# Squares summed in a tree on VectorE, one ones-matmul for a chunk, in the front of a hybrid encoder layer

## What is computed

```python
def rms_norm(x, g, eps=NORM_EPS):
    xf = x.astype(jnp.float32)
    y = xf * lax.rsqrt(jnp.mean(xf * xf, axis=-1, keepdims=True) + eps)
    return (y * g.astype(jnp.float32)).astype(x.dtype)

hn = rms_norm(x, g_pre_mix)
z, xbc, dt_raw, q, k, v = jnp.split(hn @ w_in, IN_SPLITS, axis=-1)
xbc, conv_new = causal_conv(conv_buf, xbc, conv_w, conv_b)
...
mn = rms_norm(mem, g_mem)          # 256 rows
mk, mv = mn @ wk_x, mn @ wv_x
```

## Time and profile before

| | |
|---|---|
| median of three runs | 2197.03 us |
| the profiled execution | 2196.18 us, its span 2194.4 us |
| TensorE matmul busy | 2009.8 us (92% of the span), granted clock 0.946 on average |
| VectorE busy | 924.7 us (42%) |
| ScalarE busy | 508.1 us (23%) |
| GpSimd busy | 438.5 us (20%) |
| the chain that ended last | TensorE 78%, VectorE 14%, ScalarE 3%, DMA 2% |

### The profile page before, as it was taken

How to read it: one execution, slowest core, us unless ns; L and a number is a source line. 1 busy time by engine, 2 the same in 40 slices (tenths; PEclk the granted TensorE clock), 3 DMA queues, 4 the chain that set the end, 5 groups by cost and what they waited for, 6 DMA issues and landing times.

```text
span 2194.4 us, 29435 instructions
## 1 busy us (share of the span) xinstructions
PE 2009.8 (92%) x12084; PEld 1910.8 (87%) x12084; DVE 924.7 (42%) x1673; ACT 508.1 (23%) x1078; POOL 438.5 (20%) x211
## 2 busy tenths in 40 slices
PE   8989989995988799898989978999999999999996
PEld 7988979995676698797879958999999999999995
DVE  3753176672777425503433452313322322331336
ACT  5322212323555322312322322010010000001002
POOL 0000011130000042131004213332341431433330
PEclk9999999996599899999989988999999999999998
DMA  5133222124002410013320121111110110110132
GB/s 179 58 121 106 89 89 85 62 79 149 1 1 89 166 39 30 19 58 141 128 87 29 58 87 39 39 39 39 39 52 27 49 48 21 58 39 30 49 106 86
DMA packets 63045, 148.71 MB, mean 68 GB/s; under 512 B 4288, under 2 KB 34368, under 8 KB 61376
## 3 DMA queue, kind: packets, MB, share of 16 engines
q1 hardware_dynamic: 33952, 103.53, 14.0%
q10 hardware_dynamic: 28960, 43.24, 5.7%
HBM read 123.31 MB, written 23.44 MB: 67 GB/s over the span
## 4 chain that ended last, share of the span: by engine, by line
PE 78%; DVE 14%; issue 3%; ACT 3%; DMA 2%; ACTq 0%; SPq 0%; DVEq 0%
PE bank L198 22%; PE bank L202 21%; PE bank L201 21%; PE bank L249 3%; DVE at_sm L1858 2%; DVE NLf L258 2%; PE bank L964 2%; PE bank L975 1%; DVE acc L1629 1%; PE bank L934 1%; DMA qkr<-out_k 1%; DVE ATT L1877 1%; DVE hid_l L2085 1%; PE bank L843 1%; PE bank L641 1%
## 5 line engine op out<-in xcount | busy, mean ns | idle before, releaser
L201 PE MATMUL bank<-NL,w_hi 128*128 128x384 f32 x1800 | 610.9, 339 | 0.0
L198 PE MATMUL bank<-NH,w_hi 128*128 128x384 f32 x1608 | 549.3, 342 | 36.7 <-DVE hr L2083 12.4
L202 PE MATMUL bank<-NH,w_lo 128*128 128x384 f32 x1608 | 545.0, 339 | 0.0
L483 POOL TENSOR_TENSOR w_hi<-w_raw,one 128x1024 fp32r<-128x1024 f32 x90 | 183.4, 2038 | 1219.2 <-PE bank L198 1097.2
L201 PEld LDWEIGHTS bank<-NL,w_hi 128*128 128x128 f32 x1800 | 342.0, 190 | 1.5
L198 PEld LDWEIGHTS bank<-NH,w_hi 128*128 128x128 f32 x1608 | 305.2, 190 | 40.4 <-DVE hr L2083 13.0
L202 PEld LDWEIGHTS bank<-NH,w_lo 128*128 128x128 f32 x1608 | 305.2, 190 | 0.0
L485 POOL TENSOR_TENSOR w_lo<-w_raw,w_hi 128x1024 fp32r<-128x1024 f32 x90 | 228.4, 2538 | 7.1
L2083 DVE TENSOR_TENSOR hr<-sg,bank 128x384 f32<-128x384 f32 x66 | 36.6, 554 | 433.3 <-PE bank L202 433.3
L198 PE MATMUL bank<-hid_h,w_hi 128*128 128x384 f32 x528 | 179.0, 339 | 16.0 <-DVE ACC L2094 14.6
L2094 DVE TENSOR_TENSOR ACC<-ACC,bank 128x384 f32<-128x384 f32 x240 | 131.8, 553 | 115.8 <-PE bank L202 115.8
(11 more groups left out here) (319 smaller groups left out, 2941.2 us busy)
## 6 DMA issues: line engine op xcount, KB each, us to landing
w_raw<-in_wall SPq DMA_DIRECT2D x130, 512.0 KB, 3.3
cK<-in_cmk SPq DMA_DIRECT2D x8, 1024.0 KB, 7.0
cV<-in_cmv SPq DMA_DIRECT2D x8, 1024.0 KB, 5.0
H<-in_xT SPq DMA_DIRECT2D x5, 1536.0 KB, 12.5
scratch_h<-H ACTq DMA_DIRECT2D x3, 1536.0 KB, 6.0
Hback<-scratch_h ACTq DMA_DIRECT2D x3, 1536.0 KB, 10.5
out_y<-Hback ACTq DMA_DIRECT2D x3, 1536.0 KB, 6.0
Kb<-in_kc SPq DMA_DIRECT2D x6, 512.0 KB, 9.0
```

The source lines that it names most:

```text
L198: m = mm(out, ah, bh, start=(i == 0), stop=False)
L201: mm(out, ah, bl, start=False, stop=False)
L202: m = mm(out, al, bh, start=False, stop=(i == n - 1))
L483: pool.tensor_tensor(whi[s][:], raw[s % 2][:], bc(one[:, 0:1], [P, WI]), ALU.mult).then_inc(w_hi, 1)
```

## The change

The eight squares of a chunk are no longer summed by eight accumulating ones-matmuls. `front_sum` adds them on VectorE, in place, in a tree of three additions (4 + 4 blocks, 2 + 2, 1 + 1), and `front_pe` issues one ones-matmul on the block that is left. This is done for the three chunks of x and for the memory; the norms later in the program keep `pre_pe`. A new semaphore (`norm_front_sum`) joins the tree to the ones-matmul; a few unused names of semaphores go.

```diff
+        def front_sum(dve, p, w):
+
+            dve.wait_ge(n_sq, 4 * p + 4)
+            s = g("msq" if p == P_MEM else f"fsq{p % 2}")
+            for n in (4, 2):
+                dlink(dve, TT(s[:, 0:n, 0:w], s[:, 0:n, 0:w], s[:, n:2 * n, 0:w], ALU.add))
+            TT(s[:, 0, 0:w], s[:, 0, 0:w], s[:, 1, 0:w], ALU.add).then_inc(n_sum, 1)
+
+        def front_pe(pe, p, w):
+
+            pe.wait_ge(n_sum, p + 1)
+            if p:
+                pe.wait_ge(n_std, p)
+            mm(B[7][:, 0:w], ones[:, :], g("msq" if p == P_MEM else f"fsq{p % 2}")[:, 0, 0:w], start=True,
+               stop=True).then_inc(n_pc, 4)
...
                 if c:
-                    pre_pe(pe, P_MIX + c - 1, NC)
+                    front_pe(pe, P_MIX + c - 1, NC)
...
                         if m == 2 and c == 0:
-                            pre_pe(pe, P_MIX + 2, NC)
+                            front_pe(pe, P_MIX + 2, NC)
                         if m == 2 and c == 1:
-                            pre_pe(pe, P_MEM, MEM)
+                            front_pe(pe, P_MEM, MEM)
...
             weight_low(dve, 2)
-            n_low(2)
+            front_sum(dve, P_MIX, NC)
+            x_low(2)
             weight_low(dve, 3)
+            front_sum(dve, P_MIX + 1, NC)
+            front_sum(dve, P_MIX + 2, NC)
...
             conv(0)
             weight_low(dve, 5)
+            front_sum(dve, P_MEM, MEM)
             pre_dve(dve, P_MEM, g("mraw"), g("mraw")[:], g("mlo")[:], g("mhi")[:], G_MEM, MEM)
```

More of the change, by code:

```diff
@@ L162, in build @@
         ld_x0 = [sem(f"ld_x0_{i}") for i in range(2)]
-        s_past = sem("conv_past")
+        s_past, n_sum = sem("conv_past"), sem("norm_front_sum")
         w_raw = [sem(f"w_raw_in{i}") for i in range(2)]
@@ L370, in build @@
         a_lo, a_oc, b_kn, b_pn = sem("att_qk_low"), sem("att_out"), sem("smp_new_keys"), sem("smp_new_values")
-        a_tr, a_tre, a_S, a_nb, a_exp, a_att, a_T, a_Te, a_pv, a_o, a_on, a_yt, a_yte = (
+        a_tr, a_tre, a_S, a_nb, a_exp, a_att, a_T, a_Te, a_pv, a_on, a_yt, a_yte = (
             sem("att_" + n) for n in ("qk_trans", "qk_copy", "scores", "max", "exp", "probs", "ptrans", "pcopy", "pv",
-                                      "ocopy", "onorm", "otrans", "oout"))
+                                      "onorm", "otrans", "oout"))
         ld_kb = [sem(f"ld_kc{i}") for i in range(DB // 2)]
-        b_q, b_S, b_nb, b_exp, b_p, b_T, b_Te, b_pv, b_o, b_ot, b_ote = (
-            sem("smp_" + n) for n in ("qbd", "scores", "max", "exp", "probs", "ptrans", "pcopy", "pv", "ocopy", "otrans",
-                                      "otok"))
+        b_q, b_S, b_nb, b_exp, b_p, b_T, b_Te, b_pv, b_o = (
+            sem("smp_" + n) for n in ("qbd", "scores", "max", "exp", "probs", "ptrans", "pcopy", "pv", "ocopy"))
         x_qh, x_ql, mk_h, mk_l = (sem("x_" + n) for n in ("q_high", "q_low", "k_high", "k_low"))
@@ L1574, in _, with x_low @@
             dve.wait_ge(ld["vec"], 16)
-            def n_low(c):
+            def x_low(c):
                 for i in range(4):
@@ L1584, in _ @@
             weight_low(dve, 0)
-            n_low(0)
+            x_low(0)
             weight_low(dve, 1)
-            n_low(1)
+            x_low(1)
             weight_low(dve, 2)
-            n_low(2)
+            front_sum(dve, P_MIX, NC)
+            x_low(2)
             weight_low(dve, 3)
+            front_sum(dve, P_MIX + 1, NC)
+            front_sum(dve, P_MIX + 2, NC)
             dve.wait_ge(ld["row"], 16)
```

## The result

The changed kernel takes 2205.71 us (median of its runs, 2202.03 to 2215.01), the kernel before 2197.0 in the same rounds: ratio 1.0041, 95% interval 1.0029 to 1.0054. I had forecast 2192.4, at most 2197.6. The profiled execution took 2205.78 us (span 2204.0). One of the sixteen executions took 3542.77 us at a granted clock of 0.765; it is left out of the range and of the ratio and hardly moves the median.

A forecast was written before the change was run, and what follows sets the result against it. The front was taken as bound by TensorE up to chunk 2's root, then by VectorE's queue to 114.60. Shift 4.3 + clock 0.3 = 4.6 us: profiled 2196.18 becomes 2191.6, median 2192.4 us; range 2188.0 to 2197.6.

The forecast's parts named there:

- VectorE's part: Additions put into VectorE's queue: some 3.3 us a tree, 2.4 for the memory's, 12.4 us for all four.
- Step by step: Front traced through TensorE, ScalarE and VectorE: root of chunk 2 8.7 us earlier, memory's norm 4.3 us earlier.
- The wait that the change adds: Behind the memory's tree, VectorE has nothing for 2.0 us during ones-matmul, ScalarE steps and hand-overs; TensorE waits 10.6 us before.
- Does TensorE become late: Before x5: TensorE still waits for the low part, some 2 us instead of 6.2, so the 4.3 us reach 114.60.
- The clock: TensorE's half clock behind the pause at 114.60 and two later pauses; balance put at 0.3 us gained.
- rival B: Behind 114.60 the clock stays up, so 3.0 us come back too: 7.3 us gained, 2189.7 us; chance 0.20.
- The failed step: After 114.60, loads, splits and matmuls start each other, so the 4.3 us shift stays to the end.
- Rival D: Slower: memory's tree and wait, 4.4 us on VectorE's queue, not earned back; 2201.4 us, about 2203 with half clock; chance 0.09.
- The chain of waits in the front, because the change touches nothing later: What the prediction examined for the bound: waits up to 114.60, where TensorE has 6.2 us of slack beside VectorE's queue.

The follow-up runs named there:

- run 1: Changed kernel plus eight always-met waits (four instructions) on TensorE before the memory's ones-matmul; 2180.39 us, ratio to the kernel before 0.9913.
- run 6: Changed kernel plus 223 met waits (111 instructions), so the feed-forward loop begins at the same instruction number as in the kernel before; 2188.49 us, ratio 0.9947.
- run 7: Changed kernel plus 144 met waits (72 instructions), so the loop begins 70 instructions behind the start of a 16 KB piece; 2189.74 us, ratio 0.9959.
- run 2: Kernel before plus met waits in two TensorE pauses, so the loop begins 253 instructions behind a 16 KB piece's start; 2213.55 us, ratio 1.0064.
- run 5: Kernel before plus 299 met waits (149 instructions), so the loop begins 2 instructions behind a 16 KB piece's start; 2182.38 us, ratio 0.9932.
- run 8: Kernel before plus 156 met waits (78 instructions), so the loop begins 187 instructions behind a 16 KB piece's start; 2197.47 us, ratio 1.0004.
- run 4: Kernel of run 1 with the memory's tree on VectorE moved ahead of conv(0); 2174.22 us, ratio to the kernel before 0.9894.

## Why the prediction was wrong, point by point

- **VectorE's part: right.** A tree of 3.3 us and one of 2.4 for the memory, as forecast to a tenth.
- **Step by step: right to within 1 us on ScalarE and VectorE.** The load of the memory is issued at 40.87 (forecast 40.1), the root of chunk 2 is there at 50.2 (49.9), and the norm of the memory stands at 64.12 (63.5), 3.7 us early for 4.3. TensorE's pauses are shorter than forecast, 2.22 us before x2 (3.0) and 8.74 before the memory's ones-matmul (10.6), and the clock behind the longer one cost 2.9 us (7.1 us at 0.59) for at most 2.5; 5.4 us at 0.50, from which I had that bound, are already 2.7. The wait that the change adds is paid where I put it.
- **Does TensorE become late: right.** It still waits before x5, 1.20 us for some 2.
- **The clock: the term was too small.** I put its balance at 0.3 us. The profiled execution got back 3.0 us behind x5 and 1.7 behind the pause that stood at 183.0, which is rival B's way and more. It is a toss, though: the changed kernel's front was 9.2 us ahead at 194 us, in runs 1, 6 and 7, with the same front, 6.6, 7.6 and 7.1. The kernel before is as unsteady there: in runs 2, 5 and 8, with its own front, it is 2.9 us ahead, 0.8 late and 2.1 late. At place 109 the change is worth 8.9 us in the medians (run 6; 7.7 to 15.6 by the interval of its ratio), near rival B's 7.3 and twice the 4.6 of the forecast. The kernels at 253 and 254 differ by 7.8 us (2213.55 and 2205.71), those at place 2 by 2.0 alone (2182.38 and 2180.39, with ranges that overlap), so 8.9 is not its worth at every place.
- **The failed step** is the sentence "From there on all loads, splits and matmuls are started by each other, so the shift stays to the end." It looked at semaphores only. At the loop's turns TensorE waits for none, it waits for its own instructions, and the removal of 111 instructions moved the loop from place 109 to 254. That costs 17.2 us (2205.71 against 2188.49). The -8.9 and the +17.2 add up to the measured loss by their making, since both are taken against run 6. What bears out the second is run 2: there the move alone, from 109 to 253 in the kernel before, cost 15.9 us (2213.55 against 2197.65). The shift does not quite stay even without the move: in run 6's execution 8.9 us at the loop's first turn are 4.5 at the end.
- **Rival D** gave the right sign and nearly the right size, but by another mechanism (the tree and the wait not earned back); that did not happen, and the nearness is luck. "The chain of waits in the front, because the change touches nothing later" was the look that hid the real one: the view of waits of the kernel before has four waits of TensorE for "issue" at the loop's turns, 2.4 to 2.7 us each, and the range should have held what becomes of them when the program gets shorter.

## What to carry to other kernels

Where TensorE waits for "issue" at a loop's turn and a packet of the instruction queue falls into the pause, it may be waiting for its instructions. Then any edit ahead of the loop, even of code that runs once, can change that wait: here it was nothing, 2.3 to 3.2 or 4.9 to 6.3 us a turn. Look at the instruction queue's packets in that stretch of both kernels before a difference is put down to the edit, and compare at the same instruction number of the loop. A handful of instructions that do nothing, in a pause, may be worth more than the edit: here four of them brought 25 us, the edit 8.9.

## What the runs showed that I had not expected

- A loop of 1802 instructions can go through four turns without one packet of instructions (run 4) or with nine a pass, by its place alone.
- A pause of 2.35 us left the clock at 0.52 in run 6, one of 2.41 us left it at 1.00 in the kernel before. The lengths do not tell them apart.
- With one and the same program the executions of run 1 spread over 19 us, those of run 4 over 8. The clock's stretches and the fetches at the turns fall differently each time, so a gain of a few microseconds is not to be read from one profiled execution.
